# One wide product of values for two heads: 256 moving columns in place of twice 128 in the prompt's attention

## What is computed

```python
def sink_attention(q, k, v, allowed, sinks):
    s = jnp.einsum('...thgd,...khd->...hgtk', q, k).astype(jnp.float32) * (A_HEAD_DIM ** -0.5)
    s = jnp.where(allowed, s, -jnp.inf)
    ...
    p = e / (jnp.sum(e, axis=-1, keepdims=True) + jnp.exp(sink - mx))
    return jnp.einsum('...hgtk,...khd->...thgd', p.astype(v.dtype), v)
```

## Time and profile before

| | us |
|---|---|
| median of 3 runs | 1515.64 |
| lowest, highest | 1515.54, 1517.97 |
| span of the profiled execution | 1514.5 |
| TensorE busy in it | 1367.6 |
| TensorE weight loads | 860.2 |
| VectorE, ScalarE busy | 351.1, 252.6 |

### The profile page before, as it was taken

One profiled execution on the slowest core, in us unless ns is written; L12 is line 12 of the kernel. 1 busy time (PEld: TensorE's weight loads), 2 busy tenths in 40 slices (PEclk: granted clock), 3 DMA queues, 4 the chain that ended last, 5 costly groups with the idle time before them and its releaser, 6 DMA issues.

```text
span 1514.5 us, 22807 instructions
## 1 busy us (share of the span) xinstructions
PE 1367.6 (90%) x9764; PEld 860.2 (57%) x9765; DVE 351.1 (23%) x938; ACT 252.6 (17%) x558; POOL 31.4 (2%) x69
## 2 busy tenths in 40 slices
PE   9999999999999999888888888888888889999996
PEld 7878888888888543433423333333333356666665
DVE  3312221036721411301201010101010112222227
ACT  3201121041401321111101111111101111111015
POOL 1000000020022000000000000000000000000000
PEclk9999999999999999989979998989988999999998
DMA  9556333377988799999999999999999999999981
GB/s 347 201 170 226 123 127 114 142 276 270 370 299 364 287 427 418 426 427 427 427 426 428 429 429 428 428 428 428 429 428 429 428 385 426 427 427 428 426 350 58
DMA packets 64640, 527.50 MB, mean 348 GB/s; under 512 B 6030, under 2 KB 27926, under 8 KB 29350
## 3 DMA queue, kind: packets, MB, share of 16 engines
q1 hardware_dynamic: 63182, 525.27, 84.7%
q10 hardware_dynamic: 1384, 1.16, 0.2%
HBM read 512.33 MB, written 14.07 MB: 348 GB/s over the span
## 4 chain that ended last, share of the span: by engine, by line
DMA 43%; PE 26%; DVE 1%; issue 1%; ACT 0%; DVEq 0%; ACTq 0%; SPq 0%
DMA raw<-in_w_up 26%; PE ps L1944 7%; DMA more<-in_w_down_cuts 4%; DMA raw<-in_w_down_cuts 4%; PE ps L154 4%; PE ps L2208 4%; PE ps L2182 4%; DMA more<-in_w_up 4%; DMA more<-in_w_down 4%; DMA more<-in_w_gate_cuts 1%; PE ps L1184 1%; PE ps L1968 1%; PE ps L2192 1%; PE ps L1919 1%; PE ps L1957 1%
## 5 line engine op out<-in xcount | busy, mean ns | idle before, releaser
L154 PE MATMUL ps<-mixT_hT,raw 128*128 128x264 f32 x1920 | 436.1, 387 | 2.9 <-PEq L808 1.7
L154 PEld LDWEIGHTS ps<-mixT_hT,raw 128*128 128x128 f32 x1920 | 361.6, 190 | 68.0 <-issue 7.4
L1944 PE MATMUL ps<-raw,mixT_hT 128*32 128x512 f32 x1488 | 205.3, 683 | 91.4 <-DMA raw<-in_w_up 61.0
L1944 PEld LDWEIGHTS ps<-raw,mixT_hT 128*32 128x32 f32 x1488 | 43.0, 116 | 216.7 <-DMA raw<-in_w_up 91.1
L2208 PE MATMUL ps<-mixT_hT,more 128*128 128x264 f32 x512 | 126.3, 395 | 1.2 <-DMA more<-in_w_gate_cuts 1.2
L1199 DVE TENSOR_TENSOR mixT_hT<-ps,ffn_gain 128x512 f32<-128x512 f32 x33 | 22.8, 691 | 424.1 <-PE ps L1919 424.1
L2208 PEld LDWEIGHTS ps<-mixT_hT,more 128*128 128x128 f32 x512 | 93.9, 190 | 33.6 <-issue 19.7
L1184 PE MATMUL ps<-x_res,mine 128*32 128x512 f32 (+1 forms) x792 | 108.2, 664 | 0.3 <-DVE mine L1622 0.3
L1957 PEld LDWEIGHTS ps<-fold,mixT_hT 128*128 128x128 f32 x512 | 70.5, 213 | 53.9 <-issue 37.7
L1957 PE MATMUL ps<-fold,mixT_hT 128*128 128x32 f32 x512 | 77.8, 299 | 5.8 <-ACT mixT_hT L1766 5.8
L1919 PEld LDWEIGHTS ps<-ident,xe 128*64 128x64 f32 x1056 | 66.5, 217 | 27.2 <-issue 27.2
(11 more groups left out here) (373 smaller groups left out, 890.5 us busy)
## 6 DMA issues: line engine op xcount, KB each, us to landing
raw<-in_w_gate SPq DMA_DIRECT2D x62, 2048.0 KB, 16.5
raw<-in_w_down_cuts SPq DMA_DIRECT2D x35, 2048.0 KB, 18.4
more<-in_w_up SPq DMA_DIRECT2D x32, 2048.0 KB, 15.8
raw<-in_w_up SPq DMA_DIRECT2D x31, 2048.0 KB, 17.1
raw<-in_mix_chunks SPq DMA_DIRECT2D x60, 1024.0 KB, 5.5
more<-in_w_down SPq DMA_DIRECT2D x16, 2048.0 KB, 23.8
more<-in_w_down_cuts SPq DMA_DIRECT2D x13, 2048.0 KB, 26.2
more<-in_w_gate_cuts SPq DMA_DIRECT2D x8, 2048.0 KB, 21.8
```

Source lines behind the costliest of these rows:

```text
L154: return nc.tensor.matmul(ps[:, j, 0:NT], core.raw[:, q % NCH, k * GW + j * P:k * GW + (j + 1) * P], xT[:, core.groups[g].k0 + c * CK + k, ...
L1944: last = nc.tensor.matmul(ps[own, (GATE, UP)[m], :], xT[:, k, i * SLOTS:(i + 1) * SLOTS], weights, start=(i == 0 and k < 4), stop=(i == EI ...
```

## The change

In `values`, the two heads whose output goes to the same half of the partitions are served by one matmul. It has the same stationary operand, a moving operand of two slots of `prT` that lie four slots apart (heads par and par + 2 for one key block), and it writes the columns 0 to 255 of bank 6. A unit of the first block has 2 matmuls where it had 4, a unit of the second block 4 where it had 8: 24 in all in place of 48. The halves come one after the other: first all matmuls of the lower half, then all of the upper. Nothing else differs; waits and semaphores are as before.

```diff
@@ -589,12 +589,11 @@
             def values(u):
                 g, b = divmod(u, 2)
                 pe.wait_ge(q["a_turned"], u + 1)
-                for i in range(4):
-                    lo = (i % 2) * HD
+                for par in range(2):
+                    lo = par * HD
                     for kb in range(b + 1):
-                        last = nc.tensor.matmul(ps[lo:lo + HD, 6, (i // 2) * P:(i // 2 + 1) * P],
-                                                avtok[:, kb, g * HD:(g + 1) * HD], prT[:, i * 2 + kb, :],
-                                                start=(kb == 0), stop=(kb == b))
+                        last = nc.tensor.matmul(ps[lo:lo + HD, 6, 0:2 * P], avtok[:, kb, g * HD:(g + 1) * HD],
+                                                prT[:, 2 * par + kb::4, :], start=(kb == 0), stop=(kb == b))
                 last.then_inc(q["a_pv"], 1)
```

## The result

| | median, us | lowest to highest | runs |
|---|---|---|---|
| before | 1515.64 | 1514.17 to 1518.9 | 13 |
| after | 1518.91 | 1516.06 to 1522.48 | 13 |

The ratio is 1.0020, with a 95% interval of 1.0013 to 1.0028. The change costs 3.3 us by the medians and 3.0 by the ratio; the forecast was 0.24 us saved, and the time lies outside the range.

The account below looks back on a forecast made before the run. TensorE was taken to bound the attention, with savings there starting the expert weight stream earlier; DMA bounds from 735 us. Savings of 4 x 0.06 + 4 x 0.00 = 0.24 us gave 1515.64 - 0.24 = 1515.4 us, range 1513.8 to 1517.6.

Parts of the forecast that it names:

- the 0.42 us of the columns: Attention scores: 128 more columns in each of four rounds cost 0.42 us, 0.105 us a round.
- the distances 0.59 and 1.02: Values, L595's first start to the next line's: 0.59 us in first-block units, 1.02 in second-block units after the change.
- the pairs 0.01 us apart: Values: the first two records of a unit should start 0.01 to 0.02 us apart.
- the loads and the semaphore worth nothing: Values: 48 fewer weight loads of 137 ns are worth 0; `a_pv` rises as before and no new wait opens.
- Rival 2: Values: a moving operand in two pieces reads slower, 1.6 us (cheap form, chance 0.04) or 6.4 us (dear, 0.02).
- its dear form: Values: the two-piece operand's extra cost grows with the columns, 6.4 us, giving 1521.6 us; chance 0.02.
- Rival 1: Values: in strict queue order the upper half waits for the lower half's last start; 3.4 us more, 1518.8 us; chance 0.05.
- the 0.24 us: Values: total saving, 0.06 us in each of four second-block units, 0.00 in the first-block ones, reaching the end in full.
- The prediction's last sign: Whole kernel: the forecast is wrong about the end if the distances hold but the median moves by over 1.6 us.
- that is everything that the change can touch: Attention: all eight units' products of values together take 6.7 us, 0.44% of the span, the most the change can affect.
- The 0.03 left "for what I don't see": Whole kernel: chance of 0.03 left for runs that scatter and for effects not seen.
- From 735 us on the DMA engines are full ... there nothing that TensorE saves counts: Expert stretch from 735 us: DMA share 1.01 at 428 GB/s, TensorE has room, so its savings there are worth nothing.

Follow-up runs that it names:

- e4: The kernel before with heads in the order 0, 2, 1, 3, still 128 columns and 48 matmuls; ratio 1.0015 to the kernel before.
- e2: The changed kernel with 190 waits (96 instructions) added in a branch that is not taken; ratio 1.0000 to the kernel before, median 1515.72 us.
- e1: The changed kernel once more, no edit; ratio 1.0021 to the kernel before, median 1519.95 us.
- e5: The changed kernel with 86 waits (44 instructions) added in the branch that is not taken; ratio 1.0035 to the kernel before, median 1521.33 us.
- e8: The changed kernel with TensorE's last stage right behind the expert loop and a second copy behind the passes' code; ratio 0.9992 to the kernel before, 1514.90 us.
- e3: The kernel before with 318 waits (160 instructions) added in the branch that is not taken; ratio 1.0013 to the kernel before, median 1518.62 us.

## Why the prediction was wrong

The working in the attention held in each number: the 0.42 us of the columns, the distances 0.59 and 1.02, the pairs 0.01 us apart, the loads and the semaphore worth nothing. Rival 2 was wrong in both forms: the rounds are 0.22 us apart with the moving operand in two pieces, behind a first of 0.27 (0.16 with 128 columns). The price of its dear form should read 1515.4 + 6.4 = 1521.8 us and not 1521.6; nothing rests on it. Rival 1's rule, strict order, isn't what these traces show, but neither is a half's queue endless: four records (e4). That the 0.24 us would reach the end one for one is not shown: unit 0's values start at 119.38 us before and 119.82 us after, so that much differs between the profiles ahead of any saving. The prediction's last sign came true as written: the distances as said, the median moved by over 1.6 us, and something behind the attention had changed.

Three steps failed.

The first is the sentence "that is everything that the change can touch". It counted executed work. The change also took 96 instructions out of the program, and with them moved all code behind; with the code moved back (e2) the ratio is 1.0000 instead of 1.0021. The 0.03 left "for what I don't see" was the only room for that, and the range closed at 1517.6.

The second is "From 735 us on the DMA engines are full ... there nothing that TensorE saves counts". It rested on one row up to 1200 us. The rows from 1200 to 1240 us show 388 GB/s where 428 is full: 3.7 us of loading lost (40 x (1 - 388 / 428)), because TensorE comes late to the last stage. The same reckoning gives 4.7 us in the changed kernel, 7.0 in e1 (353), 8.1 in e5, 1.4 in e2 and 0.2 in e8. With the target at the same place it differs by 2.3 us from profile to profile (the kernel before and e2, the changed kernel and e1), so one profile gives the size only to some 2 us, and the medians have to carry it. At this change of stage TensorE sets the pace, and I hadn't looked at it.

The third follows: "issue", 4.8 us at L2182, was in the list of waits of the kernel before. I took it for a given, when it was the largest single wait that TensorE had in that stretch and depends on where code lies.

How 2.1 us of waiting become 3.0 to 3.3 us at the end is only partly shown. The granted clock is half of full speed (1.2 GHz) in most of this stretch, and in this pair it stays so longer where TensorE stands longer: 0.56 of full speed from 1217.30 to 1223.57 us before, 0.52 from 1214.72 to 1224.50 us after:

```profile
1217.30:1223.57 6.27, 6.27 (x64) 3.16 (x64) 0.00 (x0) 0.38 (x1) 0.00 (x0) 0.56 0.72 233
```

```profile
1214.72:1224.50 9.78, 7.70 (x64) 3.21 (x64) 0.00 (x0) 0.38 (x1) 0.00 (x0) 0.52 0.79 293
```

So the first 64 records run partly at half speed as well as with a stop in them. In the profiled pair the stream of loads is 1.2 us late behind this place (its 500th MB starts at 1415.5 and at 1416.7 us), of which 0.3 us was there ahead of the stage (385th MB, 1141.9 and 1142.2 us); the span is 2.7 us longer, and the rest arises at the very end, where another load came last than before. No run separates that from scatter.

## What to carry to other kernels

Where a program jumps, the end of the time can hang on the count of instructions, not only on what they do: before judging an edit that adds or removes many, look for waits for "issue" behind each jump, and repeat the comparison with padding in code that is never executed. Put the code that always runs right behind the loop, and the exception behind it. And where the loads set the pace on average, read the stretches around each change of stage by themselves: the row of the mean hides the places where another engine sets it.

## What the runs showed of the hardware

- At a forward jump over 1610 instructions (by the count in the program) TensorE waits 4.6 to 5.1 us for "issue"; its next matmul comes 3.3 to 3.8 us later than without the jump (5.7 to 6.15 us after the last L1956 group's start, against 2.35). The next block after the target's comes 5.6 to 6.2 us behind the target's (4.35 in e3). TensorE stands a second time with 8, 52 and 116 instructions left in the target's block (4.60; 2.07, 2.22 and 0.73; 0.65 us), and not with about 212.
- With the array divided in halves by output columns, the lower half holds four records (a float32 matmul is two), and then the queue behind it stops for both halves: in e4 the upper half starts 0.005 us after the lower half's fifth record. With four records ahead it starts 0.01 us after the first, at 128 columns and at 256.
- A source of the scatter between runs: in the profiled executions of e3 and e4 the granted clock fell at 515 to 517 us, where TensorE sets the pace, and SyncE issues the load of 589.88 us 4.0 and 3.8 us late, at 593.84 and 593.66 us. From 514 to 528 us, the kernel before and then e3:

```profile
514.00:528.00 14.00, 12.91 (x118) 6.26 (x119) 4.15 (x18) 4.67 (x7) 0.00 (x0) 1.00 1.01 359
```

```profile
514.00:528.00 14.00, 12.88 (x86) 6.05 (x89) 3.71 (x16) 2.79 (x5) 0.00 (x0) 0.63 0.75 266
```
